# A decoder step on one core: the memory's K/V projection computed inside the dilated attention's loop, with sixteen row buffers

## The reference

```python
def mem_project(mem, w_mem_kv_l):            # 256 x 1024 @ 1024 x 512
    return (mem @ w_mem_kv_l).reshape(mem.shape[0], mem.shape[1], 2, MEM_HEADS, HEAD_DIM)

def dilated_prompt(q, k, v, window, dil):    # three groups: (128,1), (512,4), (2048,16), 4 heads of 64
    ...
    s = jnp.einsum('brnqhd,brnkhd->brnhqk', qs, kb).astype(jnp.float32) * ATTN_SCALE
    s = jnp.where(mask[None, None, :, None], s, -jnp.inf)
    lse = jax.nn.logsumexp(s, axis=-1)
    p = jnp.exp(s - lse[..., None])
    o = jnp.einsum('brnhqk,brnkhd->brnqhd', p.astype(vb.dtype), vb)
```

## Time and profile before

| | us |
|---|---|
| median of 3 runs | 2304.71 (2299.87 to 2311.17) |
| the profiled execution | 2307.14, its span 2305.4 |
| TensorE busy | 2114.3 (92% of the span) |
| VectorE / ScalarE / GpSimd busy | 1175.4 / 621.3 / 518.2 |
| mean granted TensorE clock | 0.943 |
| `attend_window` | 743.1 to 862.2 of the span |
| `mem_project` | 862.2 to 889.75 |

### The profile page before, as it was taken

The page is one execution under the profiler, slowest core; times in us unless marked ns, Lnnn a source line. Parts: engine busy times, 40 slices in busy tenths (PEclk is TensorE's granted clock), DMA queues, the critical chain, the costliest instruction groups (busy, mean ns, idle before and its releaser), DMA issues. The chain is left out here.

```text
span 2305.4 us, 32999 instructions
## 1 busy us (share of the span) xinstructions
PE 2114.3 (92%) x12535; PEld 1945.7 (84%) x12535; DVE 1175.4 (51%) x2287; ACT 621.3 (27%) x1247; POOL 518.2 (22%) x569
## 2 busy tenths in 40 slices
PE   5999899999998976898669989989999999999997
PEld 5878788999998864555359988889999999999997
DVE  5049999998720413542337232644344444444445
ACT  5243222121210752343122233631121111111112
POOL 4786656778820001100000120210000000000000
PEclk9999999999986966999789998999999999999999
DMA  4122222357632444871337202030112110111001
GB/s 154 28 85 75 66 85 82 110 165 250 210 122 88 124 136 126 253 261 59 96 100 203 65 29 73 19 110 22 53 56 56 37 55 20 55 56 55 19 10 76
DMA packets 201025, 215.90 MB, mean 94 GB/s; under 512 B 47958, under 2 KB 186230, under 8 KB 200358
## 3 DMA queue, kind: packets, MB, share of 16 engines
q1 hardware_dynamic: 173206, 156.56, 23.1%
q10 hardware_dynamic: 26624, 29.87, 3.7%
q0 software_dynamic: 1040, 27.33, 3.5%
HBM read 178.94 MB, written 62.10 MB: 105 GB/s over the span
## 5 line engine op out<-in xcount | busy, mean ns | idle before, releaser
L3088 PE MATMUL p_g<-n_t_hi,g_hi 128*128 128x352 f32 x1056 | 342.4, 324 | 11.8 <-DVE g_lo L2980 8.9
L3088 PE MATMUL p_g<-n_t_lo,g_hi 128*128 128x352 f32 x1056 | 341.9, 324 | 0.0
L3088 PE MATMUL p_g<-n_t_hi,g_lo 128*128 128x352 f32 x1056 | 341.7, 324 | 0.0
L935 PE MATMUL pz<-w_hi,n_hi 128*128 128x384 f32 (+2 forms) x720 | 245.8, 341 | 0.4 <-issue 0.4
L935 PE MATMUL pz<-w_hi,n_lo 128*128 128x384 f32 (+2 forms) x720 | 239.6, 333 | 0.0
L935 PE MATMUL pz<-w_lo,n_hi 128*128 128x384 f32 (+2 forms) x720 | 239.4, 333 | 0.0
L3088 PEld LDWEIGHTS p_g<-n_t_hi,g_hi 128*128 128x128 f32 x1056 | 199.4, 189 | 13.0 <-issue 11.5
L843 DVE MATCH_REPLACE8 sel<-m,sel 128x1024 f32<-128x1024 f32 (+4 forms) x224 | 205.3, 921 | 0.0
L3088 PEld LDWEIGHTS p_g<-n_t_lo,g_hi 128*128 128x128 f32 x1056 | 199.4, 189 | 0.0
L3088 PEld LDWEIGHTS p_g<-n_t_hi,g_lo 128*128 128x128 f32 x1056 | 199.4, 189 | 0.0
L840 DVE MAX8 m<-sel 128x8 f32<-128x1024 f32 (+4 forms) x224 | 197.5, 925 | 0.2
(11 more groups left out here) (408 smaller groups left out, 4286.8 us busy)
## 6 DMA issues: line engine op xcount, KB each, us to landing
w_raw<-in_w_in SPq DMA_DIRECT2D x26, 768.0 KB, 4.6
relu<-z_qb SPq DMA_DIRECT2D x24, 512.0 KB, 5.2
w_first<-in_w_ffn_in SPq DMA_DIRECT2D x22, 512.0 KB, 6.7
g_raw<-in_w_ffn_in SPq DMA_DIRECT2D x22, 512.0 KB, 4.7
o_raw<-in_w_ffn_out SPq DMA_DIRECT2D x22, 512.0 KB, 4.1
z_b<-z ACTq DMA_DIRECT2D x48, 192.0 KB, 1.9
gates<-z ACTq DMA_DIRECT2D x48, 176.0 KB, 2.8
gate<-gates SPq DMA_DIRECT2D x24, 352.0 KB, 3.9
```

The lines of the kernel that those rows point to most:

```text
L935: m = pe.matmul(out, tokens(a, k, i), b[:, n % 2, k, 0:w], start=(k == 0 and p == 0), stop=(k == KC - 1 and p == 2))
L3088: m = pe.matmul(p_g[:, t, e, 0:THIRD], a[:, u, e, w], b[:, k, t * THIRD:(t + 1) * THIRD], start=(k == 0 and p == 0), stop=(k == KC - 1 and ...
```

## The change

`mem_project` is deleted, and its work is laid into the turns of `attend_window` as 14 side jobs. `SIDE` binds each to the window job before whose `values` it is computed; all of them use the right half of the bank `p_o`. Kind m (jobs 3 to 10) transposes one eighth of the memory, kind z (jobs 13, 14, 18, 20) is one quarter of the projection in 24 matmuls of 256 columns, kind t (jobs 16, 17) turns half of K. VectorE takes a side job out four turns after the job's logits (`take_side`, behind `soft`), for kind m with a rounding copy and a subtraction, and splits one eighth of the weight in each of the turns 8 to 15 (`split_weight`). The row ring has sixteen slots; memory and weight are loaded among the first row loads; the mask is loaded behind the first rows. The core of the diff:

```diff
-BR, OR = 7, 5
+BR, OR = 16, 5
+SIDE = {3 + k: ("m", k, 0) for k in range(KC)}
+SIDE.update({13: ("z", 0, 0), 14: ("z", 1, 0), 16: ("t", 0, 0), 17: ("t", 1, 0), 18: ("z", 0, 1), 20: ("z", 1, 1)})
+SIDE_NO = {j: n + 1 for n, j in enumerate(sorted(SIDE))}
+SPLIT_FROM = 8
...
+        p_side = p_o[:, 256:512]
...
             def _(sp):
-                sp.dma_start(ident[:, :], d["ident"]).then_inc(s_const, 16)
-                sp.dma_start(masks[:, :], d["att_mask"]).then_inc(s_const, 16)
+                sp.dma_start(ident[:, :], d["ident"]).then_inc(s_ident, 16)
                 for j in range(NB_J):
                     g, u = B_JOBS[j]
+                    if j == 1:
+                        sp.dma_start(masks[:, :], d["att_mask"]).then_inc(s_mask, 16)
+                    if j == 6:
+                        sp.dma_start(m_in[:, :, :], d["mem_prompt"].rearrange("(i p) c -> p i c", p=P)).then_inc(s_min, 16)
+                    if j == 9:
+                        sp.dma_start(w_raw[:, :, :], d["w_mem_kv"][0].rearrange("(k p) c -> p k c", p=P)).then_inc(s_wraw, 16)
                     if j >= BR:
                         sp.wait_ge(s_pv, j - BR + 2)
...
+                for half, kept in enumerate((k_row, vm)):
+                    for i in range(2):
+                        sp.wait_ge(s_side, SIDE_OF[("z", i, half)])
+                        sp.dma_start(d["new_mem_kv"][i * P:(i + 1) * P, 256 * half:256 * half + 256], kept[:, i, :]).then_inc(s_new, 16)
...
             def _(dve):
+                def split_weight(k):
+                    dve.wait_ge(s_wraw, 16)
+                    dve.tensor_copy(w_hi[:, k, :], w_raw[:, k, :]).then_inc(s_whi, 1)
+                    dve.wait_ge(s_whi, k + 1)
+                    dve.tensor_tensor(w_lo[:, k, :], w_raw[:, k, :], w_hi[:, k, :].bitcast(F32), ALU.subtract).then_inc(s_wlo, 1)
+
+                def take_side(j):
+                    kind, a, b = SIDE[j]
+                    dve.wait_ge(s_oev, j + 1)
+                    if kind == "m":
+                        dve.tensor_copy(m_hi[:, a, :], p_side).then_inc(s_mhi, 1)
+                        dve.wait_ge(s_mhi, a + 1)
+                        dve.tensor_tensor(m_lo[:, a, :], p_side, m_hi[:, a, :].bitcast(F32), ALU.subtract).then_inc(s_side, 1)
+                    elif kind == "z":
+                        dve.tensor_copy((vm if b else k_row)[:, a, :], p_side).then_inc(s_side, 1)
+                    else:
+                        dve.tensor_copy(km_t[:, a, :], p_side).then_inc(s_side, 1)
...
                 for it in range(NB_J + 2):
                     if it < NB_J:
                         soft(it)
+                    if it - 4 in SIDE:
+                        take_side(it - 4)
+                    if 0 <= it - SPLIT_FROM < KC:
+                        split_weight(it - SPLIT_FROM)
                     if 0 <= it - 2 < NB_J:
                         take_probs(it - 2)
...
             def _(pe):
+                def side(j):
+                    kind, a, b = SIDE[j]
+                    if SIDE_NO[j] > 1:
+                        pe.wait_ge(s_side, SIDE_NO[j] - 1)
+                    if kind == "m":
+                        pe.wait_ge(s_min, 16)
+                        for i in range(2):
+                            pe.transpose(p_o[:, 256 + i * P:256 + (i + 1) * P], m_in[:, i, a * P:(a + 1) * P], ident[:, :])
+                    elif kind == "z":
+                        pe.wait_ge(s_wlo, KC)
+                        for k in range(KC):
+                            for p, (x, y) in enumerate(((m_hi, w_hi), (m_lo, w_hi), (m_hi, w_lo))):
+                                pe.matmul(p_side, x[:, k, a * P:(a + 1) * P], y[:, k, 256 * b:256 * b + 256], start=(k == 0 and p == 0), stop=(k == KC - 1 and p == 2))
+                    else:
+                        for i in range(2):
+                            pe.transpose(p_o[:, 256 + i * P:256 + (i + 1) * P], k_row[:, i, a * P:(a + 1) * P], ident[:, :])
+
                 def values(j):
                     a, b = B_JOBS[j]
+                    if j:
+                        pe.wait_ge(s_oev, j)
+                    if j in SIDE:
+                        side(j)
+                    elif j - 1 in SIDE:
+                        pe.wait_ge(s_side, SIDE_NO[j - 1])
                     pe.wait_ge(s_ptA, j + 1)
                     if second[j]:
                         pe.wait_ge(s_ptD, second[j])
-                    if j:
-                        pe.wait_ge(s_oev, j)
...
-def mem_project(nc, d, km_t, vm, m_in, w_raw):
...
-                    attend_window(nc, d, m_in, w_raw)
-                    mem_project(nc, d, km_t, vm, m_in, w_raw)
+                attend_window(nc, d, km_t, vm)
```

More of the change, by code:

```diff
@@ L1128, in block_rows, with attend_window @@
     return [(0, v[2 * u, :, :]), (64, v[2 * u + 1, :, :])]
-def attend_window(nc, d, m_in, w_raw):
+SIDE = {3 + k: ("m", k, 0) for k in range(KC)}
+SIDE.update({13: ("z", 0, 0), 14: ("z", 1, 0), 16: ("t", 0, 0), 17: ("t", 1, 0), 18: ("z", 0, 1), 20: ("z", 1, 1)})
+SIDE_NO = {j: n + 1 for n, j in enumerate(sorted(SIDE))}
+SIDE_OF = {SIDE[j]: SIDE_NO[j] for j in SIDE}
+SPLIT_FROM = 8
+def attend_window(nc, d, km_t, vm):
     ctx = ExitStack()
@@ L1146, in attend_window @@
         p_x = ps("p_x", [P, 512])
-        s_const = sem("w_const")
+        p_side = p_o[:, 256:512]
+        m_in = sb("m_in", [P, 2, D])
+        m_hi = sb("m_hi", [P, KC, 2 * P], F32R)
+        m_lo = sb("m_lo", [P, KC, 2 * P], F32R)
+        w_raw = sb("w_mem_raw", [P, KC, 512])
+        w_hi = sb("w_hi5", [P, KC, 512], F32R)
+        w_lo = sb("w_lo5", [P, KC, 512], F32R)
+        k_row = sb("k_row5", [P, 2, 256])
+        s_ident = sem("w_ident")
+        s_mask = sem("w_mask")
+        s_min = sem("w_min")
+        s_wraw = sem("w_wraw")
+        s_whi = sem("w_whi")
+        s_wlo = sem("w_wlo")
+        s_mhi = sem("w_mhi")
+        s_side = sem("w_side")
+        s_new = sem("w_new")
         s_brow = [sem(f"w_brow{u}") for u in range(BR)]
-        s_mem = sem("w_mem")
         s_xt = sem("w_xt")
@@ L1186, in _ @@
                         sp.dma_start(b_row[p0:p0 + src.shape[0], j % BR, :], src).then_inc(s_brow[j % BR], 16)
-                sp.dma_start(m_in[:, :, :], d["mem_prompt"].rearrange("(i p) c -> p i c", p=P)).then_inc(s_mem, 16)
-                sp.dma_start(w_raw[:, :, :], d["w_mem_kv"][0].rearrange("(k p) c -> p k c", p=P)).then_inc(s_mem, 16)
+                for half, kept in enumerate((k_row, vm)):
+                    for i in range(2):
+                        sp.wait_ge(s_side, SIDE_OF[("z", i, half)])
+                        sp.dma_start(d["new_mem_kv"][i * P:(i + 1) * P, 256 * half:256 * half + 256], kept[:, i, :]).then_inc(s_new, 16)
                 for j in range(NB_J - OR, NB_J):
                     sp.wait_ge(s_ob[j % OR], stored_b[j])
-                sp.wait_ge(s_mem, 32)
+                sp.wait_ge(s_new, 64)
             @block.scalar
@@ L1262, in take_probs @@
                     dve.tensor_copy(probs_t[:, j % 2, 512:w], p_t[:, 1, 0:w - 512]).then_inc(s_ptD, 1)
-                dve.wait_ge(s_const, 32)
+                def split_weight(k):
[14 more added lines that the diff above has]
+                        dve.tensor_copy(km_t[:, a, :], p_side).then_inc(s_side, 1)
+                dve.wait_ge(s_mask, 16)
                 for it in range(NB_J + 2):
@@ L1321, in values @@
                     m.then_inc(s_pv, 1)
-                pe.wait_ge(s_const, 32)
+                pe.wait_ge(s_ident, 16)
                 for it in range(LAST):
@@ L3148, in run_phases @@
                 vm = inv_ffn[:, 4 * P:8 * P].rearrange("p (c k) -> p c k", c=2)
-                with ExitStack() as loaded:
-                    m_in = on(loaded, "m_in", [P, 2, D])
-                    w_raw = on(loaded, "w_mem_raw", [P, KC, 512])
-                    attend_window(nc, d, m_in, w_raw)
-                    mem_project(nc, d, km_t, vm, m_in, w_raw)
+                attend_window(nc, d, km_t, vm)
                 oa = [on(mixers, f"oa_{x}", [P, 4, T], F32R) for x in ("hi", "lo")]
```

## The result

The changed kernel takes 2292.64 us (median of 16 runs, 2283.35 to 2301.78) against 2304.59 for the kernel before (16 runs): the ratio is 0.9942, with a 95% interval of 0.9927 to 0.9957, or 13 us less (10 to 17). The forecast was 2295.7, within 2285 to 2305. The profiled execution has a span of 2294.0 us instead of 2305.4.

What follows compares the result with a forecast made beforehand. Wide turns were taken as bound by TensorE, with the projection stage as the prize. -27.0 + 14.0 + 0.25 - 1.0 = -13.8, plus 5 for the clock, gave -9 us: median 2295.7, range 2285 to 2305.

Steps and rivals of the forecast that it cites:

- What is removed: The memory's projection stage, 27.55 us, goes; 0.55 is kept for opening the next stage: 27.0 us less.
- the tail: The stretch from 849.6 to 862.2, at the low clock before, gets 1 us back (0 to 2).
- The new wait: Turns 7 to 14: values wait until VectorE, behind `soft`, empties the shared bank; 2.43 us in wide turns, 1.89 in narrow.
- The side work: On TensorE: two transposes take 0.25 us; 24 matmuls of 256 columns take 2.9 us.
- Turns 15 to 23: Summed turn by turn at full clock, with z jobs and some waits behind VectorE: 43.8 us together.
- The floor of 3.85: Turns 19 and 22 take 3.85 us each, half of 7.70, taken for ScalarE's pace.
- The start: Turn 6 adds 0.25 us; a gain of a few tenths from the mask behind the first rows was left out.
- The clock: New TensorE idle times in turns 7 to 14 bring two to three falls of its granted clock: 5 us more.
- rival 1: The clock holds through the turns, so nothing is lost to falls: -14 us, 2291; chance 0.20.
- Rival 3: VectorE's pass is off the path and TensorE alone counts: -29 us, 2276; chance 0.05.
- Rival 4: Hidden work comes out (late `o_b` stores, dearer z, dearer hand-offs): gain 0 to 5 us, 2302; chance 0.15.
- Rival 2: Turns 7 to 14 run at the low clock throughout: +7 us, 2312; chance 0.08.

Runs made afterwards that it cites:

- e5: The changed kernel run again unaltered, on another chip: median 2288.83 us, ratio 0.9927 to the kernel before; stage 130.7 us, clock 1.00 in turns 7 to 14.
- e3: The changed kernel with VectorE taking the side job out ahead of `soft`: median 2272.14 us, ratio 0.9863 to the kernel before; stage 117.3 us.
- e9: The changed kernel with one more VectorE copy per turn 7 to 14 and TensorE's idle time filled by repeated transposes: 2291.27 us, ratio 0.9942 to the kernel before.
- e1: The kernel before with sixteen row slots instead of seven and nothing else: median 2296.27 us, ratio 0.9973; stage 138.7 us.
- e7: The changed kernel with one more 256-column copy in VectorE's pass in turns 7 to 14: 2301.81 us, ratio 0.9984 to the kernel before; those turns 52.3 us.
- e10: Repeat of the changed kernel with one more VectorE copy in turns 7 to 14, unfilled: 2301.13 us, ratio 0.9993 to the kernel before; those turns 59.2 us.
- e8: The changed kernel with take-out ahead of `soft` and eight output-row slots instead of five: 2275.38 us, ratio 0.9859 to the kernel before; stage 117.3 us.
- e4: The changed kernel with the `turn_probs` transposes done twice in turns 7 to 14: 2287.15 us, ratio 0.9922 to the kernel before; those turns 43.2 us.
- e12: One more execution of the changed kernel with `turn_probs` transposes done twice in turns 7 to 14: 2294.33 us; stage 130.9 us.
- e11: One more execution of the changed kernel unaltered, its third profile: 2288.72 us; stage 131.9 us, turns 7 to 14 43.5 us.

## Why the prediction was right

The mechanism was right: the pass on TensorE's path, its length, and what the deleted stage gives back all came as described. The closeness of the total is in part luck. Held against the stage of the first profile, the forecast had -8.8 us and the profile shows -11.0: behind turn 23 it had 28.0 less and got 27.2, for the start 0.25 more and got 1.0 less, for turns 7 to 23 a loss of 19.0 with the clock's 5 and got 17.2. So the errors are 0.8, -1.2 and -1.8 us. The other two profiles of the same kernel show a stage 15.9 and 14.7 us shorter. And 2292.64 lies just below 2293.2, from which on the forecast speaks of faster: it gave that 0.34, and 0.61 to a change within 0.5%.

**What is removed** was put at 27.0 us, and the tail behind turn 23 at 1.0; together they became 27.2 shorter. Of the 1 us that the tail was to win by a better clock hardly anything came (12.93 less the 0.55 for the opening, against 12.58): the mean clock there was still only 0.63.

**The new wait.** The pass was worked out as 2.43 in a wide turn and measured 2.44. e5's turns 7 to 14 took, in order, 6.18, 5.11, 6.18, 5.11, 5.28, 5.11, 5.29 and 4.93 against the 6.25, 5.17, 6.25, 5.17, 5.41, 5.17, 5.41 and 4.92 of the sum: 43.2 against 43.75. e3 shows that it is the pass, and e9 what a longer pass costs.

**The side work.** 24 matmuls of 256 columns were put at 2.9 us. The first and the last of one z, and what follows:

```profile
832.93 0.36 PE L1372 MATMUL p_o<-w_hi,m_hi 128*128 128x256 f32 x1 [0.40 <-issue]
833.12 0.28 PE L1372 MATMUL p_o<-w_hi,m_lo 128*128 128x256 f32 x1
...
835.76 0.28 PE L1372 MATMUL p_o<-w_lo,m_hi 128*128 128x256 f32 x1
835.88 1.00 PE L1392 MATMUL p_o<-b_row,probs_t 128*128 128x64 f32 x8
```

From 832.93 to 835.88 is 2.95 us, 0.12 apart. Two transposes took 0.24.

**Turns 15 to 23** were put at 43.8 and took 42.7. The floor of 3.85 for turns 19 and 22 was wrong by 1.8 together: they took 2.74 and 3.14. It was read as ScalarE's pace from two turns in which TensorE was busy all of the time at the lower clock (7.70 of 7.70 us, ScalarE 5.23), so it was TensorE's pace; e1, without any side work, has a turn 19 of 2.51 us. On the other side turn 23 took 5.49 instead of 4.85: the transposes of `turn_probs` stand 0.2 and 0.4 us behind the work ahead of them at its start and its end, each time until 0.07 us after ScalarE's copy of the probabilities (L1242) has ended. And turn 16 was 0.35 longer. TensorE waits 0.36 there for VectorE's copy of the probabilities:

```profile
825.19 0.63 PE L1356 MATMUL p_t<-ident,probs 128*128 128x128 f32 x4 [0.36 <-DVE probs_t L1291]
```

Turn 15 has no wait for VectorE any more, so the splitting of the weight is not covered in it: the few tenths named for that case.

**The start** was put at 0.25 longer and was 1.0 shorter. The first rows come 0.8 us sooner (5.8 against 6.6 of waiting), more than the few tenths that I left out, and that holds in every profile with the new order of loads: the first transposes begin 3.7 to 4.0 us into the stage, against 4.57 in the kernel before and 4.65 in e1. What is left of it at `logits(7)` is less firm: these kernels need 31.3 to 32.8 us up to there, the kernel before 32.9 in its one profile, and e1, with the old order, 31.9.

**The clock** was put at two to three falls and 5 us. The first profile has two stretches at the lower clock in these turns and 4.9 us over e5. That it need not happen I gave 0.20, as rival 1; two more profiles, of one execution each, show no fall. So forecast and rival 1 are both outcomes of the same kernel, one stage of 135.6 and others of 130.7 and 131.9, and the median lies between: 2292.6, 3 us below the forecast of 2295.7 and 2 above rival 1's 2291. The mechanism of this term stood (e9). Its size was probably high as a mean, and rival 1's chance of 0.20 low, but three profiles cannot say how often the clock falls; what decides it was not found. The Trainium skill's rule ("TensorE: Matmul & The Clock Gate", section "Why this matters for your kernels") warns only of gaps longer than any of these, and to go by it alone would have misled here: idle times of up to 1.4 us, repeated each turn, went with falls in one of three profiles, and those of up to 1.7 us (e7, e10) in both.

**Rival 3** (the pass off the path) was held against the program order, and e3 shows both: it was false for this change and true for one with two lines exchanged. Its estimate for that, 29 us less than before, is what e3 measures in the stage (146.6 to 117.3) and by its ratio (32 us, 24 to 39). **Rival 4** is out: stores hidden (e8), z as priced, and the hand-offs as reckoned (the pass of 2.44 us). **Rival 2**, the low clock throughout, never came in the changed kernel, but e10 with its idle times 0.33 us longer is near to it (a mean clock of 0.69): a stage of 147.8 us, longer than before.

## What to carry to other kernels

When work moves into a loop, the engine that takes its result out matters more than the engine that does it: find the point in that engine's order where the result is ready, and put the take-out there, not behind a step that itself waits for the engine being held up. Here the order of two calls on VectorE was worth 13 to 18 us in the stage, about as much as the whole change (11 to 16). A buffer shared by two users makes such an order a wait; so reckon every turn as a sum of what must follow what, which in turns 7 to 14 came out within 0.13 us a turn. And more slots in one ring can lay bare the next ring's waits, as those for `o_b` in e1.

## What was not expected of the hardware

TensorE's clock answers to idle times that are short and repeated, and not the same way each time. The same program had a mean granted clock of 0.86, 1.00 and 1.00 in the same turns, with idle times of 0.9 to 1.4 us; 0.33 us more in each turn gave 0.82 and 0.69. Useless transposes in the idle time brought it back to 1.00 and saved 6.5 us or more.

A single execution's span is a coarse measure here. The code ahead of the stage, the same in all, ended between 736.5 us (e10) and 749.0 us (e9), while the stage itself is steadier where the clock holds (130.7, 130.9 and 130.9 in e5, e4 and e12; 131.9 in e11, which took 1.3 us longer than e5 up to `logits(7)`). What varies ahead of the stage was not looked into.
